# Block 1's attention with the score tiles two ahead, and four places for the compressed rows

## The reference, cut to what matters

```python
def one_block(i):                       # 128 queries
    s_c = einsum('bgrqd,bgnd->bgrqn', qb, k_c) * scale
    p_c = masked_softmax(s_c, c_end[None, :] <= tpos[:, None])
    o_c = einsum('bgrqn,bgnd->bgrqd', p_c, v_c)
    s_s = einsum('bgrqd,bgqkd->bgrqk', qb, ks_g) * scale
    p_s = masked_softmax(s_s, m_s[:, :, None])
    o_s = einsum('bgrqk,bgqkd->bgrqd', p_s, vs_g)
    s_w = einsum('bgrqd,bgkd->bgrqk', qb, kw) * scale
    p_w = masked_softmax(s_w, m_w)
    o_w = einsum('bgrqk,bgkd->bgrqd', p_w, vw)
    return gb[..., 0:1] * o_c + gb[..., 1:2] * o_s + gb[..., 2:3] * o_w
```

## Time and profile before

| what | us |
|---|---|
| median of three runs | 2795.05 |
| the profiled execution | 2790.86 |
| its span on the core | 2789.1 |
| attention of block 1, filler of round 0 to the first dense matmul behind it | 276.01 to 498.37 |
| of it, rounds 8 to 47 | 306.84 to 444.84 |

### The profile page before, as it was taken

One profiled execution on the slowest core, in us unless ns is written; L12 is line 12 of the kernel. 1 busy time (PEld: TensorE's weight loads), 2 busy tenths in 40 slices (PEclk: granted clock), 3 DMA queues, 4 the chain that ended last, 5 costly groups with the idle time before them and its releaser, 6 DMA issues.

```text
span 2789.1 us, 38071 instructions
## 1 busy us (share of the span) xinstructions
PE 2678.1 (96%) x13128; PEld 2195.5 (79%) x13128; DVE 1568.5 (56%) x2448; ACT 1056.2 (38%) x1826; POOL 1179.2 (42%) x592
## 2 busy tenths in 40 slices
PE   8999888999999999999999999999899999999998
PEld 6877777778888878888887788888687778888886
DVE  8996666564342476476656735545623446653364
ACT  4224878623222254443324411112525553211133
POOL 3432595334444444354333344444442224444443
PEclk9999999999999999999999999999999999999999
DMA  3342000233322232221112332222231112322332
GB/s 137 99 140 83 16 24 9 65 131 100 98 98 92 96 131 84 82 94 61 54 38 95 134 98 95 94 98 95 97 104 56 46 45 91 128 97 92 98 98 90
DMA packets 67459, 242.88 MB, mean 87 GB/s; under 512 B 7771, under 2 KB 10116, under 8 KB 66572
## 3 DMA queue, kind: packets, MB, share of 16 engines
q1 hardware_dynamic: 59760, 215.37, 23.7%
q10 hardware_dynamic: 7580, 25.91, 2.7%
HBM read 232.80 MB, written 6.35 MB: 86 GB/s over the span
## 4 chain that ended last, share of the span: by engine, by line
issue 50%; PE 29%; POOL 18%; DVE 1%; ACT 1%; POOLq 1%; DVEq 0%; ACTq 0%
POOL w_lo L442 14%; PE bank L2585 7%; PE bank L2587 7%; PE bank L2586 7%; POOL stat L469 3%; PE bank L3133 2%; PE bank L3122 2%; POOL stat L466 2%; PE bank L2800 1%; POOLq L446 0%; PE bank L2771 0%; PE bank L3106 0%; PE bank L3171 0%; PE bank L3157 0%; PE bank L3109 0%
## 5 line engine op out<-in xcount | busy, mean ns | idle before, releaser
L442 POOL TENSOR_TENSOR w_lo<-raw,w_hi 128x1024 fp32r<-128x1024 f32 x398 | 972.7, 2444 | 1541.7 <-ACT w_hi L589 1420.7
L2585 PE MATMUL bank<-act,w_hi 128*128 128x512 f32 x3128 | 1259.6, 403 | 51.1 <-POOL w_lo L442 15.2
L2587 PE MATMUL bank<-act,w_lo 128*128 128x512 f32 x3128 | 1227.5, 392 | 0.0
L2586 PE MATMUL bank<-act,w_hi 128*128 128x512 f32 x3128 | 1226.3, 392 | 0.0
L589 ACT CAST w_hi<-raw 128x1024 fp32r<-128x1024 f32 x396 | 415.7, 1050 | 898.0 <-PE bank L2587 887.4
L2585 PEld LDWEIGHTS bank<-act,w_hi 128*128 128x128 f32 x3128 | 592.2, 189 | 198.7 <-issue 32.5
L2587 PEld LDWEIGHTS bank<-act,w_lo 128*128 128x128 f32 x3128 | 592.1, 189 | 127.2
L2586 PEld LDWEIGHTS bank<-act,w_hi 128*128 128x128 f32 x3128 | 593.0, 190 | 121.3 <-issue 5.7
L1685 DVE TENSOR_TENSOR X<-X,bank 128x512 f32 x56 | 38.5, 687 | 241.3 <-PE bank L2587 241.3
L2076 DVE CAST act<-tmp 128x512 f32 x64 | 142.5, 2226 | 10.0 <-DVE tmp L2072 5.2
L1837 DVE SCALAR_TENSOR_TENSOR bank<-big,cols,bank 128x512 f32<-128x512 f32 x174 | 117.1, 749 | 0.4
(11 more groups left out here) (427 smaller groups left out, 2957.6 us busy)
## 6 DMA issues: line engine op xcount, KB each, us to landing
raw<-in_w_dram SPq DMA_DIRECT2D x402, 512.0 KB, 3.4
act_f<-head_rows ACTq DMA_DIRECT2D x8, 768.0 KB, 4.4
proj_rows<-big ACTq DMA_DIRECT2D x4, 1024.0 KB
big<-proj_rows ACTq DMA_DIRECT2D x2, 2048.0 KB, 9.0
X<-in_x_dram SPq DMA_DIRECT2D x4, 512.0 KB, 6.1
act_f<-in_cw1k_dram ACTq DMA_DIRECT2D x4, 512.0 KB, 4.3
cst<-in_consts_dram ACTq DMA_DIRECT2D x2, 648.5 KB, 7.7
X<-big ACTq DMA_DIRECT2D x8, 128.0 KB, 4.0
```

The lines of the kernel that those rows point to most:

```text
L442: pool.tensor_tensor(w_lo[:, u], raw[:, u].rearrange("p (k n) -> p k n", k=KT), w_hi[:, u].bitcast(F32), ALU.subtract).then_inc(w_lo_ready, 1)
L2585: pe.matmul(o, l_hi, r_hi, start=start, stop=False)
L2586: pe.matmul(o, l_hi, r_lo, start=False, stop=False)
L2587: return pe.matmul(o, l_lo, r_hi, start=False, stop=stop)
```

## The change

Nothing is computed differently. In code: TensorE takes two score tiles ahead instead of one, and the second compressed score of a pair in round 1 of a group instead of round 2. ScalarE takes the exponentials of tile n+1 ahead of the scaling of tile n, and the second compressed exponential in round 3 instead of 4. VectorE takes the maxima of tile n+2 instead of n+1, and the second compressed shift in round 2 instead of 3. The compressed rows of a head go to one of four places instead of two; the two new ones lie in `CW2K`, whose contents are no longer needed then, and get their padding column cleared once each. The semaphores and what they protect are the same, except that a shift waits for the transpose of four heads back instead of two.

```diff
         CW2K = region(2 * P).rearrange("p (c d) -> p c d", c=2)
+        PC_ROWS = (PC_ROWS[:, 0], PC_ROWS[:, 1], CW2K[:, 0], CW2K[:, 1])
...
+        def compressed_rows(h):
+
+            return PC_ROWS[h % 4].rearrange("p (q n) -> p q n", q=TT)[:, :, 0:NCMP]
...
                     if n >= 2:
                         keep_pt(n - 2)
+                    if n + 1 < N:
+                        exps(n + 1)
                     if n < N:
                         scale_rows(n)
...
-                    if n % 8 in (2, 4) and n // 8 + 1 < NH // 2:
-                        compressed_exp(n // 8 * 2 + 2 + (n % 8 == 4))
-                    if n + 1 < N:
-                        exps(n + 1)
+                    if n % 8 in (2, 3) and n // 8 + 1 < NH // 2:
+                        compressed_exp(n // 8 * 2 + n % 8)
...
+                    if h in (2, 3):
+                        link(v.memset(CW2K[:, h - 2].rearrange("p (q n) -> p q n", q=TT)[:, :, NCMP:], 0.0))
                     link(v.tensor_reduce(CST, sc, AX.X, ALU.max))
-                    if h >= 2:
-                        v.wait_ge(tr_done, (h // 2 - 1) * 8 + h % 2 + 1)
-                    v.tensor_tensor(PC[:, h % 2, :, 0:NCMP], sc, per_row(CST), ALU.subtract).then_inc(c_shifted, 1)
+                    if h >= 4:
+                        v.wait_ge(tr_done, (h // 2 - 2) * 8 + h % 2 + 1)
+                    v.tensor_tensor(compressed_rows(h), sc, per_row(CST), ALU.subtract).then_inc(c_shifted, 1)
...
                 maxima(0)
+                maxima(1)
...
-                    if n + 1 < N:
-                        maxima(n + 1)
+                    if n + 2 < N:
+                        maxima(n + 2)
                     if n // 8 + 1 < NH // 2:
-                        if n % 8 in (1, 3):
-                            compressed_shift(n // 8 * 2 + 2 + (n % 8 == 3))
+                        if n % 8 in (1, 2):
+                            compressed_shift(n // 8 * 2 + n % 8 + 1)
...
                 scores(0)
+                scores(1)
                 for n in range(N + 2):
                     if n < 6 * KT:
                         gate_filler(n)
-                    if n + 1 < N:
-                        scores(n + 1)
-                    if n % 8 in (0, 2) and n // 8 + 1 < NH // 2:
-                        compressed_scores(n // 8 * 2 + 2 + (n % 8 == 2))
+                    if n + 2 < N:
+                        scores(n + 2)
+                    if n % 8 in (0, 1) and n // 8 + 1 < NH // 2:
+                        compressed_scores(n // 8 * 2 + 2 + n % 8)
```

More of the change, by code:

```diff
@@ L996, in compressed_exp @@
                     a.wait_ge(c_shifted, h + 1)
-                    a.activation(PC[:, h % 2, :, 0:NCMP], PC[:, h % 2, :, 0:NCMP], ACT.Exp).then_inc(c_exp, 1)
+                    a.activation(compressed_rows(h), compressed_rows(h), ACT.Exp).then_inc(c_exp, 1)
                 compressed_exp(0)
@@ L1951, in compressed_shift @@
                     sc = bank[5][:, at:at + TT * NC2].rearrange("p (q n) -> p q n", q=TT)[:, :, 0:NCMP]
+                    if h in (2, 3):
+                        link(v.memset(CW2K[:, h - 2].rearrange("p (q n) -> p q n", q=TT)[:, :, NCMP:], 0.0))
                     link(v.tensor_reduce(CST, sc, AX.X, ALU.max))
-                    if h >= 2:
-                        v.wait_ge(tr_done, (h // 2 - 1) * 8 + h % 2 + 1)
-                    v.tensor_tensor(PC[:, h % 2, :, 0:NCMP], sc, per_row(CST), ALU.subtract).then_inc(c_shifted, 1)
+                    if h >= 4:
+                        v.wait_ge(tr_done, (h // 2 - 2) * 8 + h % 2 + 1)
+                    v.tensor_tensor(compressed_rows(h), sc, per_row(CST), ALU.subtract).then_inc(c_shifted, 1)
                 def compressed_sum(h):
-                    to, rows = CMP_FACTOR[:, h % 2], PC[:, h % 2, :, 0:NCMP]
+                    to, rows = CMP_FACTOR[:, h % 2], compressed_rows(h)
                     v.wait_ge(c_exp, h + 1)
@@ L2890, in transposes @@
                         pe.wait_ge(c_scaled, h + 1)
-                        pe.transpose(bank[0][:, P:2 * P], PC_ROWS[:, h % 2], ident)
+                        pe.transpose(bank[0][:, P:2 * P], PC_ROWS[h % 4], ident)
                     for j in range(2):
```

## The result

The changed kernel takes 2810.35 us, the median of four executions (2809.53 to 2812.06); the kernel before took 2794.99 us beside it. The ratio is 1.0059, with a 95% interval from 1.0047 to 1.0071. The change makes the kernel slower, by 15.4 us; I had forecast 7.35 us slower and a range up to 2810.0. The time lies 0.35 us outside it, and almost on the price of the rival that I had given 0.08, slower through the clock (2810.9 us).

The account below looks back on a forecast made before the run. TensorE, busy 96% of the span, was taken as the bound, so only its waits count. Rounds 8 to 47 +6.5, group 0 +0.5 and +0.2, group 6 +0.45, group 7 -0.3: +7.35, 2802.4 us; range 2795.5 to 2810.

Parts of the forecast that it names:

- slower through the clock: Rival: new hold's idle time lowers TensorE's granted clock in each of five groups, +8.5 us, 2810.9 us; chance 0.08.
- The term of round 7: Value products wait for ScalarE's copy, 1.1 us against 1.55 before: -0.45 us a group.
- the signs that I had named: Wrong if L2874 waits under 1 us or rounds 5 and 7 under 1.4; clock under 0.9 favours slower through the clock.
- The wait that goes: VectorE's shift no longer waits 9.1 us for transposes, thanks to four row places; worth nothing by itself.
- The wait that comes: Round 1: TensorE's second compressed score waits for VectorE's first shift, 1.55 us in each of 7 groups.
- Round 3: TensorE waits 0.6 to 0.7 us, with the second shift ahead of VectorE's copies: +0.3 us a group.
- Round 5: Value products wait for VectorE's copy, 0.9 us, 1.1 with GpSimd's holds, against 1.16 before: -0.1 us a group.
- The sum: Rounds 8 to 47: five groups at 1.55 + 0.3 - 0.1 - 0.45 = +1.3, so +6.5 us; total +7.35 us.
- Groups 0, 6 and 7: Outside rounds 8 to 47: group 0 +0.5 and +0.2 us for clearings, group 6 +0.45, group 7 -0.3.
- C's wait for R: ScalarE's scaling waits for VectorE's row factor, 0.68 us in one group's rows; the exchange was to remove it.
- The rival of slack: Rival: waits of rounds 5 and 7 fall to 0.5 us each, giving +1.4 us, 2796.4 us; chance 0.22.

Follow-up runs that it names:

- e2_comp_only: Kernel before with only the change's compressed part (second score, shifts and second exponential a round sooner, four row places), one tile ahead: 2817.83 against 2795.12 us.
- e1_shift_01: Changed kernel with both compressed shifts in rounds 0 and 1 of VectorE's group instead of 1 and 2: 2789.25 us, kernel before 2795.12 us.
- e12_sums_later_only: Changed kernel with only VectorE's compressed sums moved, from rounds 4 and 6 to 5 and 7: 2796.05 us, kernel before 2793.45 us.
- e4_comp_behind_values: Changed kernel with the second compressed score behind the products with the values in round 1, not ahead: 2794.97 us, kernel before 2795.12 us.
- e9_sums_later: Changed kernel with shifts in rounds 0 and 1, compressed sums in 5 and 7, finished heads' copy ahead of maxima: 2785.76 us, kernel before 2793.84 us.
- e7_narrow_taps_after: Changed kernel with GpSimd's convolution taps 8 columns wide instead of 512: 2793.95 us, kernel before 2793.84 us.
- e5_fill_hold: Changed kernel with twelve unread matmuls of 256 columns ahead of the second compressed score in round 1: 2805.94 us, kernel before 2795.12 us.

## Why the prediction was wrong

Two steps failed. The term of round 7 was to be -0.45 us a group, released by ScalarE; it came out at +0.11, released by VectorE. And the clock, which stood in no term of the sum, cost 4.3 to 4.8 us in rounds 8 to 47. Of the signs that I had named, neither of those for a wrong forecast came (L2874 waits 1.30 us, R5 and R7 together 2.86 us a group); the clock row under 0.9, the sign of the third rival, did.

The table has the waits of TensorE per group in rounds 8 to 47, means of five, in us.

| place | before | forecast | after |
|---|---|---|---|
| R1, hold (start distances) | 0 | 1.55 | 1.47 |
| R3 | 0.39 | +0.3 | 0.62 |
| R5 | 1.16 | -0.1 | 1.20 |
| R7 | 1.55 | -0.45 | 1.66 |
| busy time, clock included | 24.49 | 0 | 25.75 |

- **The wait that goes** was worth nothing, as said: no row after shows a gain from it. No run has the four places alone; in `e2_comp_only` they come with the hold.
- **The wait that comes** was right in kind, place, chain and size: one wait of L2874 for L1963 in each of the seven groups, 1.47 us against 1.55 where the earlier trace rows stood (1.30 as the profile's wait, 1.69 in group 0 and 1.59 in group 6). The first experiment removes it by its cause.
- **Round 3** was right to 0.1 us a group.
- **Round 5** came out within 0.15 us a group, by luck. I had built its 0.9 us without holds on the row at 360.04, whose wait ended with ScalarE's copy, and it was to tell VectorE's chain; 0.2 us were for GpSimd. With narrow taps R5 is 0.24 us, so some 0.96 of the measured 1.20 us goes when GpSimd's taps are narrow.
- **Round 7 is the first step that failed.** The release was to be ScalarE's, 1.1 us. It is VectorE's in four of five groups, and the mean of the five is 1.66 us. I had counted ScalarE's 4.0 us between two copies and left out VectorE's chain in the same round: a product of R, maxima, and the whole compressed sum, three instructions of which take two operands from SBUF. The earlier trace rows showed what such an instruction can take. I used that row for the moved subtraction, which is not held, and not for the sum, which stands ahead of the copy. Narrow taps show both halves: R7 falls to 0.76 us with ScalarE as its release, and the change costs some 6 us. The sums moved by themselves (`e12_sums_later_only`) show the place: R7 is 0.63 us at most. By the Trainium skill, page SBUF — State Buffer, section "SBUF: two separate sides", a VectorE instruction with two inputs in SBUF and a GpSimd instruction that reads SBUF lock a shared port pair against each other, each for its whole length; the trace agrees, with 1.39 us beside GpSimd's addition and 0.29 us without. This term is some 0.55 us a group, 2.8 us in five.
- **The chance of the clock is the second.** I put it at 0.08 because the one wait of 2.29 us had brought no fall. That was one wait in a group with little else idle. Before, a group had 3.1 us of idle time on average; after, it has 3.9 to 5.1 (its length less PE's busy time), the hold close behind the wait of round 7, and three of five groups lost clock, 1.6 us each, with one more in group 6. Filling the holds gave back 4.4 us. The rival's own sum, 8.5 us in all five groups, was too high, and its total of 2810.9 us came out right by luck, together with round 7.
- **The sum.** +14.6 in rounds 8 to 47 against +6.5. Of the 8.1 us missed, round 7 is 2.8, round 5 is 0.7, the clock 4.3 by busy time, and rounds 1 and 3 take back 0.7 us. The 1.0 us that is left is busy time that all groups have more (24.88 us where the clock was kept, against 24.49 before, of which 0.17 is the hold again, 1.47 by starts and 1.30 as a wait). By starts the clock is 4.8 us, and 0.5 us is left. Busy time is modelled, and no run separates this part.
- **Groups 0, 6 and 7**: group 0 took 1.7 us more instead of 0.7, the last two together 0.35 less instead of 0.15 more, although group 6 lost clock. The 2.7 us outside the attention between the two profiled executions are not explained by the change; the medians differ by 15.4 us and not by 18.7.
- **C's wait for R** did not vanish, as I had written it would: ScalarE's waits for L1938 are 9.7 us in 310.40 to 463.02 against 21.3 before. It cost nothing, since ScalarE waits for TensorE's transposes 39.4 us there (8.4 before). It has the slack that the change was to give. TensorE got none of it, since its waits end with VectorE.
- **The rival of slack** had the right mechanism with the wrong engine: R5 falls to nothing and R7 to 0.63 us at most once VectorE's sum is out of the way (`e12_sums_later_only`). The page Perfetto Trace Analysis of the Trainium skill, section "Optimization Strategy", advises to start dependencies sooner; the first experiment does so with the shift and gains 21 us, while the change itself, which starts the dependent score sooner than what it depends on, loses.

Open is which idle time exactly costs clock. Groups with the same waits kept it or lost it (29.86 us at 1.00, 31.48 at 0.95). In rounds 8 to 47 it was lost three times in five with the hold and the waits of R5 and R7 together (in the changed kernel and in `e2_comp_only`), once in five without the hold (`e1_shift_01` behind 2.54 us in R5, `e4_comp_behind_values` behind 1.86 us in R7, `e9_sums_later` behind 2.10 us in R6), once in five with the hold and R5 and R7 short (`e7_narrow_taps_after`), and not at all with the hold filled (`e5_fill_hold`) or with the sums later (`e12_sums_later_only`). One execution of each kernel was profiled, in the last two one of the fastest, so these are counts and not a rule.

## What to carry to other kernels

When one engine issues work a step further ahead, look in every other engine's list at what now stands behind the consumer of that work: whatever the first engine needs back from there comes late by the consumer's whole chain. Cost a wait from both engines that could release it, with the held duration of each two-operand product in the chain, and where several waits add up close together in time on TensorE, put in the clock with more than a token chance. Cost linked parts as a pair: here the exchange alone costs 24 us, and leaving it out of the full change costs 25.

## What was new about the hardware

- GpSimd's additions hold even VectorE's smallest products: 128x2 for 1.06 us (0.17 on average with narrow taps on the kernel before), 128x124 for 1.39 us (0.29 with narrow taps). Both end within 0.15 us of the end of GpSimd's instruction (366.33 behind 366.31, 368.68 behind 368.53). A subtraction of the same size with one operand in PSUM, L1963, is not held: 0.29 us on average in every kernel looked at.
- Twelve matmuls whose result nobody reads made the changed kernel 4.4 us faster in the median. In the profiled execution TensorE did not stand still for the 1.3 us of the hold, and the granted clock stayed at 1.00 in all five groups, where it had fallen in three.
- In the changed kernel the granted clock is 0.50 for some 3 us in a group that loses it, starting 1 to 2 us behind the hold, in some groups of one execution and not in others with the same waits. Other kernels lost it behind a wait of 1.86 us in R7 or of 2.54 us in R5, and the kernel before kept it behind one of 2.29 us.
